# Two layers of the second block moved, for half the tokens, into the expert stage

## The chip, the cores and the metric

The kernel runs on one core of a Trainium2 chip. TensorE (PE) multiplies, VectorE (DVE), ScalarE (ACT) and GpSimd (POOL) do the rest, and SyncE (SP) only issues transfers; each engine runs its own instructions in order, and they meet through semaphores. The metric is the device time of one execution in microseconds (us).

## The reference

256 tokens of width 1024 go through one block with attention and a product-key expert layer, a norm, and then two layers of a second block. All data are float32. What matters here:

```python
# first block, end: 128 experts for each token, drawn from tables of 16384 rows
ub = jnp.take(u_tab, ib, axis=0)
a = jnp.einsum('td,ted->te', xb, ub, preferred_element_type=jnp.float32)
w = gb * jax.nn.gelu(a, approximate=False)
vb = jnp.take(v_tab, ib, axis=0)
return jnp.einsum('te,ted->td', w.astype(vb.dtype), vb)
...
# second block, for each of two layers
h = rmsnorm_2(x, norm_g[l])
z = h @ w_in[l]                      # 1024 -> 2512
...                                  # gated linear attention (gla) and causal attention (mla) with low-rank q, k, v
x = x + jnp.concatenate([o_gla, o_mla], axis=-1) @ w_out[l]
```

Both attentions of the second block are causal: the first 128 tokens need nothing of the last 128, and the last 128 need the keys, the values and the gla state of the first.

## The kernel before

The tokens are two tiles of 128, a token to a partition. After the first block's attention comes the **expert stage**: for each tile 128 turns, in 16 groups of 8 (`GROUP`). In a turn POOL gathers, by an indirect transfer each, one row of `peer_u` and one of `peer_v` for every token (512 KB each, `gather`, L777). DVE multiplies the u row with the token and sums (`product`, L2168), and in between chooses the experts of the next two heads (`choose`). After eight products ACT takes gelu (L1006), DVE multiplies by the gates (`weights`, L2173), ACT makes eight diagonal matrices (`diagonals`, L1013), and PE adds the eight v rows, two products of 128x512 each, into two PSUM banks (`peer_group`, L1538). A float32 product is two matmul instructions, so a turn is 4 of them. The rows have buffers of their own: a set of 8 for u and 8 for v in `wring`, and from group 8 (`DEEP`) on a second set that the even groups use (`second`, L442). `u_rows` and `v_rows` issue a gather as soon as the same buffer's last row is used: one group back for groups 0 to 7, two groups back after them. POOL alternates u of group n+1 with v of group n.

When tile 0's experts are done, DVE and ACT finish its sums and norms beside the first turns of tile 1 (`finish_tile_0`). The last four v rows of all are added by DVE (`last_experts`).

Then comes the **tail**: `layer(l)` twice on every engine, both tiles together. PE's order is written out by hand: transposes of the normed rows (`zT`, L1240), the projections of `w_in` (`gqk`, L1252; `c`, `gv`, `gg`, `mg`, L1582), the low-rank products (`uq`, `ukv`, L1620, L1624), gla's chunks, the scores (`ms`, L1734, L1738), `mPT`, `mPV`, and the output product (`y2`, L1582). PE alternates the tiles, so that it has one tile's products while ACT, DVE and POOL work on the other. ACT sums squares and empties PSUM, POOL turns sums of squares into inverse roots (`inverse_rms`, L816, L820), DVE does norms, rotations, masks and residuals. The layer's weights come in eight loads on SP (`layer_chunk`) into the four places of `wring`; each waits for the last use of the load before it in its place (`LAST2`). One layer's loads are (2512 + 1024) x 1024 floats of `w_in` and `w_out`, 256 x 768 of `w_uq` and 128 x 1024 of `w_ukv`: 15.8 MB. POOL loads a layer's gains (`load_gains`), 1920 floats broadcast to 128 partitions, 0.98 MB.

## Time and profile before

| what | us |
|---|---|
| median of 3 runs (1134.6 to 1135.64) | 1134.78 |
| span of the profiled execution | 1133.4 |
| DVE's products of tile 1, first to last | about 525 to 851 |
| PE starts on the last tile's normed rows (tail) | 876.69 |
| the last product of PE ends | 1130.2 |

The table is read from the trace: times are us from the first instruction of the profiled execution. The median lies 1.4 above the span.

### The profile page before, as it was taken

The numbers are of one execution on the slowest core, as the hardware profiler recorded it, in microseconds if no ns is written. First come the engines' busy times: TensorE is split into PE (matmuls) and PEld (weight loads), VectorE is DVE, ScalarE is ACT, GpSimd is POOL, SyncE is SP. The second block draws the span as 40 slices with busy tenths as digits, with TensorE's granted clock in tenths as the row PEclk, the third lists the DMA queues.
The fourth block names the chain that finished last, engine by engine and source line by source line (L and its number), as shares of the span: only waits on it lengthen the run. The fifth ranks groups of instructions, "written<-read, shape, count | busy, mean of one in ns | idle before, by whom it ended". The sixth has DMA issues, their size and how long they took to land.

```text
span 1133.4 us, 11178 instructions
## 1 busy us (share of the span) xinstructions
PE 990.1 (87%) x3267; PEld 527.9 (47%) x3267; DVE 653.5 (58%) x1503; ACT 272.5 (24%) x741; POOL 531.0 (47%) x585
## 2 busy tenths in 40 slices
PE   4999999999997877878878688787788999999998
PEld 3858656855453323323333233332335645574454
DVE  5867776985765756756767746744444054212522
ACT  4123332222212111111141110201102364115340
POOL 1210010767777777777777777777750012000100
PEclk9999999999999998999989988889899999999999
DMA  9998855999999999999999999999999444134400
GB/s 341 315 391 319 319 203 177 381 374 408 409 409 412 410 413 413 411 413 414 412 412 414 412 410 414 414 410 414 414 410 344 154 148 124 53 121 149 149 1 38
DMA packets 123505, 361.23 MB, mean 319 GB/s; under 512 B 13400, under 2 KB 20192, under 8 KB 123328
## 3 DMA queue, kind: packets, MB, share of 16 engines
q0 software_dynamic: 75808, 275.86, 61.8%
q1 hardware_dynamic: 45280, 84.02, 20.9%
q10 hardware_dynamic: 2368, 0.76, 0.3%
q8 instruction: 22, 0.36, 0.1%
q14 instruction: 27, 0.22, 0.1%
HBM read 359.56 MB, written 1.05 MB: 318 GB/s over the span
## 4 chain that ended last, share of the span: by engine, by line
PE 46%; DMA 26%; POOL 14%; issue 7%; DVE 3%; ACT 2%; SPq 2%; POOLq 0%; DVEq 0%; ACTq 0%
PE bank L1582 14%; DMA wring<-in_peer_u,ids 12%; PE bank L1538 11%; POOL wring L777 8%; PE bank L1271 6%; DMA wring<-in_peer_v,ids 5%; POOL modb L777 3%; PE bank L1348 2%; DMA modb<-in_peer_u,ids 2%; DMA last_row<-in_peer_v,ids 2%; POOL R L777 2%; DMA wring<-in_ada_w 2%; PE bank L1252 2%; DMA wring<-in_w_in 2%; DMA R<-in_peer_u,ids 2%
## 5 line engine op out<-in xcount | busy, mean ns | idle before, releaser
L1538 PE MATMUL bank<-wring,R 128*128 128x512 f32 x496 | 245.2, 652 | 50.2 <-ACT R L1013 43.0
L2168 DVE CUSTOM_DVE_ANT_0 wring<-wring,bank 128x1024 f32<-128x1024 f32 x160 | 195.2, 1220 | 136.6 <-DMA wring<-in_peer_u,ids 135.9
L1538 PEld LDWEIGHTS bank<-wring,R 128*128 128x128 f32 x496 | 100.4, 208 | 192.6 <-issue 138.3
L777 POOL DMA_INDIRECT wring<-in_peer_u,ids x160 | 152.1, 951 | 56.5 <-issue 39.1
L777 POOL DMA_INDIRECT wring<-in_peer_v,ids x160 | 152.0, 950 | 53.0 <-issue 39.3
L1582 PE MATMUL bank<-wring,hT 128*128 128x512 f32 (+1 forms) x384 | 167.4, 589 | 3.0 <-ACT R L1202 2.5
L816 POOL TENSOR_SCALAR small<-small 128x2 f32<-128x2 f32 (+3 forms) x16 | 3.1, 192 | 307.2 <-ACTq L872 163.5
L1538 PE MATMUL bank<-R,modb 128*128 128x512 f32 x192 | 105.2, 709 | 38.6 <-ACT modb L1013 38.2
L1582 PEld LDWEIGHTS bank<-wring,hT 128*128 128x128 f32 x384 | 71.2, 190 | 83.7 <-issue 79.5
L1538 PEld LDWEIGHTS bank<-R,modb 128*128 128x128 f32 x192 | 42.6, 229 | 101.1 <-issue 55.0
L2168 DVE CUSTOM_DVE_ANT_0 modb<-modb,bank 128x1024 f32<-128x1024 f32 x48 | 58.6, 1221 | 44.3 <-DMA modb<-in_peer_u,ids 44.3
L2168 DVE CUSTOM_DVE_ANT_0 R<-R,bank 128x1024 f32<-128x1024 f32 x48 | 58.6, 1221 | 40.8 <-DMA R<-in_peer_u,ids 39.9
L1006 ACT ACTIVATE small<-small 128x8 f32<-128x8 f32 x32 | 6.7, 209 | 312.0 <-DVE small L2168 311.9
L1271 PE MATMUL bank<-hT,wring 128*128 128x256 f32 x304 | 69.8, 388 | 3.9 <-DVE small L1965 1.7
L1271 PEld LDWEIGHTS bank<-hT,wring 128*128 128x128 f32 x304 | 58.1, 194 | 13.5 <-issue 3.1
L1538 PE MATMUL bank<-wring,modb 128*128 128x512 f32 x128 | 57.8, 600 | 7.1 <-DMA wring<-in_peer_v,ids 3.7
L1013 ACT ACTIVATE modb<-const,small 128x128 f32<-128x128 f32 x128 | 39.2, 388 | 76.6 <-DVE small L2173 76.6
L1801 DVE SCALAR_TENSOR_TENSOR modb<-wring,small,modb 128x512 f32<-128x512 f32 x64 | 48.1, 752 | 14.9 <-DMA wring<-in_ada_w 11.4
L1013 ACT ACTIVATE R<-const,small 128x128 f32<-128x128 f32 x124 | 38.0, 388 | 73.0 <-DVE small L2173 73.0
L777 POOL DMA_INDIRECT R<-in_peer_u,ids x48 | 45.8, 953 | 14.6 <-issue 11.6
L777 POOL DMA_INDIRECT R<-in_peer_v,ids x48 | 45.7, 952 | 14.6 <-issue 12.2
L777 POOL DMA_INDIRECT modb<-in_peer_u,ids x48 | 45.5, 949 | 14.6 <-issue 11.9
(315 smaller groups left out, 1278.1 us busy)
## 6 DMA issues: line engine op xcount, KB each, us to landing
wring<-in_w_in SPq DMA_DIRECT2D x12, 2048.0 KB, 13.4
wring<-in_ada_w SPq DMA_DIRECT2D x8, 2048.0 KB, 13.9
...
wring<-in_w_in SPq DMA_DIRECT2D x4, 1024.0 KB, 10.5
...
wring<-in_peer_u,ids POOLq DMA_INDIRECT x160, 11.0
```

The lines of the kernel that those rows point to most:

```text
L777: pool.indirect_dma_start(dst, None, table, bass.IndirectOffsetOnAxis(index, 0)).then_inc(landed, 16)
L816: chain.step(pool.tensor_scalar(sums, sums, 1.0 / dim, EPS, ALU.mult, ALU.add))
L1006: act.activation(g8[:, b, :], a8[:, b, :], ACT.Gelu).then_inc(gelu_ready, 1)
L1013: act.activation(diag[b][:, s, :], ident, ACT.Copy, scale=w8[:, b, s:s + 1]).then_inc(diag_ready, 1)
L1252: last = pe.matmul(pb[:, o:o + P], w[:, k, a:a + P], hT[:, k, t * P:(t + 1) * P], start=k == 0, stop=k == KD - 1)
L1271: last = pe.matmul(pb[:, i * S:(i + 1) * S], w[:, k, a:a + P], hT[:, k, :], start=k == 0, stop=k == KD - 1)
L1348: last = pe.matmul(pb[:, :], hT[:, k, t * P:(t + 1) * P], w[:, k, :], start=k == 0, stop=k == KD - 1)
L1538: last = pe.matmul(pb[half][:, :], diag[b][:, s, :], v_place(n, b, s)[:, half * 512:(half + 1) * 512], start=False, stop=closing and s == ...
L1582: last = pe.matmul(pb[:, 0:n], hT[:, k, t * P:(t + 1) * P], w[:, k, wcol:wcol + n], start=k == 0, stop=k == KD - 1)
L1801: ins = dve.scalar_tensor_tensor(acc, w[:, k, :], csil[:, k:k + 1], before, ALU.mult, ALU.add)
L2168: dve.tensor_tensor_reduce(row, row, h_psum(t), 1.0, 0.0, ALU.mult, ALU.add, a8[:, b, s:s + 1]).then_inc(u_free, 1)
```

## The change

The second block's work is cut into small jobs for one tile and one layer (a "visit" `v`: 0 and 1 are tile 0's layers, 2 and 3 tile 1's). `visit_slots` puts the jobs of a visit on 50 turns, `shadow_schedule` puts visits 0 and 1 on turns 16 to 115 of tile 1's expert stage, and PE, ACT and DVE do a turn's jobs after the turn's expert work; PE's row of a turn is that of ten turns before (`LAG`). Tile 0's last sum and norm go to turns 11 to 15. `tail_schedule` is the order of visits 2 and 3, after the experts, for tile 1 alone.

The weights of both layers are now loaded twice: for visits 0 and 1 by SP into two places (`shadow_ring`) that were the second set of gather buffers, in the order `USED_BY_SHADOW`, and for visits 2 and 3 into `wring` as before. So tile 1's groups (16 and up) have one set of 8 + 8 gather buffers and wait one group back. After the front, which loads layer 0's gains as before, SP loads gains three times (layers 1, 0, 1), where POOL did once; in visits 0 and 1 the inverse roots are ACT's (`inverse_roots`, Ln and Exp), in 2 and 3 POOL's as before. Keys, values and gla's state of tile 0 are kept for tile 1. The core of the diff:

```diff
+LAG = 10
+SHADOW = 16
+VISIT = 50
...
+def visit_slots():
+
+    out = [[] for _ in range(VISIT)]
+
+    def at(r, *jobs):
+        out[r] += jobs
+
+    at(0, ("xsq",))
+    at(2, ("norm",))
+    at(3, ("zT",), ("zTe",))
+    for p in range(4):
+        at(5 + p, ("c", p))
+    at(9, ("ce",), ("gqk", 0))
+    at(10, ("gqk", 1))
+    at(11, ("cn",))
+    at(12, ("cT",), ("cTe",))
+    at(13, ("gqk", 2))
+    at(14, ("gqk", 3))
+    at(15, ("gqke",), ("gl",))
+    at(16, ("gate",), ("u", 0))
+    at(17, ("gated",), ("ue", 0))
+    at(18, ("decays",), ("u", 1))
+    at(19, ("ue", 1))
+    at(20, ("gv", 0), ("glaq",))
+    at(21, ("gv", 1), ("rope", 0))
+    at(22, ("gv", 2), ("keT",), ("rope", 1))
+    at(23, ("gv", 3), ("keR",))
+    at(24, ("gve",), ("A",), ("rope", 2))
+    at(25, ("gg", 0), ("Am",), ("rope", 3))
+    at(26, ("gg", 1), ("U",))
+    at(27, ("gg", 2), ("st",))
+    at(28, ("gg", 3), ("qkt",))
+    at(29, ("gge",), ("qkte",), ("go",))
+    at(30, ("mg", 0), ("gosq",))
+    at(31, ("mg", 1))
+    at(32, ("goe",), ("ms", 0))
+    at(33, ("mg", 2), ("mk", 0), ("mk", 1))
+    at(34, ("mx", 0), ("mx", 1), ("ms", 1))
+    at(35, ("mg", 3), ("mPT", 0))
+    at(36, ("mge",), ("mPTe", 0), ("mPT", 1), ("mk", 2), ("mk", 3))
+    at(37, ("mPTe", 1), ("mx", 2), ("mx", 3), ("mPV", 0), ("cT2", 0))
+    at(38, ("cT2e", 0), ("mPV", 1), ("mPT", 2))
+    at(39, ("mPTe", 2), ("mPT", 3), ("y2", 0, 0))
+    at(40, ("mPTe", 3), ("mPV", 2), ("y2", 0, 1))
+    at(41, ("mPV", 3), ("y2", 1, 0))
+    at(42, ("moe",), ("y2", 1, 1))
+    at(43, ("cT2", 1))
+    at(44, ("cT2e", 1))
+    at(45, ("y2", 0, 2))
+    at(46, ("y2", 0, 3))
+    at(47, ("y2", 1, 2), ("y2e", 0))
+    at(48, ("y2", 1, 3))
+    at(49, ("y2e", 1))
+    return out
+
+
+def shadow_schedule():
+
+    out = [[] for _ in range(SLOTS + LAG)]
+    for at, *jobs in ((11, ("experts", 0, 0)), (12, ("experts", 0, 1)), (13, ("final squares", 0)), (15, ("final", 0))):
+        out[at] += jobs
+    for v in range(LAYERS):
+        for r, jobs in enumerate(visit_slots()):
+            out[SHADOW + v * VISIT + r] += [(kind, v, *rest) for kind, *rest in jobs]
+    return out
+
+
+def tail_schedule():
+
+    out = []
+    for v in range(LAYERS, NT * LAYERS):
+        def to(*jobs):
+            out.extend((kind, v, *rest) for kind, *rest in jobs)
+
+        to(("xsq",), ("rms", 0), ("norm",), ("zT",), ("zTe",))
+        to(*[("c", p) for p in range(4)], ("ce",), ("rms", 1), ("cn",))
+        to(*[("gqk", i) for i in range(4)], ("cT",), ("cTe",), ("gqke",), ("gv", 0), ("gl",), ("u", 0), ("u", 1))
+        to(("gate",), ("gated",), ("ue", 0), ("ue", 1), ("rms", 2), ("decays",), ("rope", 0), ("glaq",))
+        to(*[("gv", p) for p in range(1, 4)], ("gve",), ("rope", 1), ("rope", 2), ("rope", 3))
+        to(*[("gg", p) for p in range(4)], ("gge",), ("keT",), ("keR",), ("A",), ("Am",), ("qkt",), ("qkte",))
+        to(("mg", 0), ("mg", 1), ("ms", 0), ("mk", 0), ("mk", 1), ("mx", 0), ("mx", 1), ("U",), ("st",))
+        to(("mPT", 0), ("mPTe", 0), ("mPT", 1), ("mPTe", 1), ("ms", 1), ("mk", 2), ("mk", 3), ("mx", 2), ("mx", 3))
+        to(("mg", 2), ("mPV", 0), ("mPV", 1), ("go",), ("gosq",), ("rms", 3), ("goe",), ("mPT", 2), ("mPTe", 2), ("mPT", 3), ("mPTe", 3))
+        to(("mg", 3), ("mge",), ("mPV", 2), ("mPV", 3), ("moe",), ("cT2", 0), ("cT2e", 0))
+        to(*[("y2", ch, p) for ch in range(2) for p in range(2)], ("cT2", 1), ("cT2e", 1))
+        to(("y2", 0, 2), ("y2", 0, 3), ("y2e", 0), ("y2", 1, 2), ("y2", 1, 3), ("y2e", 1))
+    return out
+
...
 
-            return b % 2 == 0 and (not isinstance(n, int) or n >= DEEP)
+            return b % 2 == 0 and (not isinstance(n, int) or DEEP <= n < NG // NT)
 
         def u_place(n, b, s):
...
                 eng.wait_ge(sems[s], 16 * (n + 1))
+            elif isinstance(n, int) and n >= NG // NT:
+                eng.wait_ge(sems[s], 16 * (n + 1 - DEEP // 2))
             else:
                 eng.wait_ge(sems[s], pair * 16 + 16 * (DEEP // 2 + 1))
...
+        shadow_ring = [region(0, 4096), region(10592, 4096)]
+        USED_BY_SHADOW = [1, 0, 3, 2, 4, 5, 6, 7]
...
+            def next_gains(v):
+
+                sp.wait_ge(gains2_used, v + 1)
+                load_gains(sp, (v + 1) % LAYERS, gains2_landed)
+
+
+            for v in range(LAYERS):
+                for j, n in enumerate(USED_BY_SHADOW):
+                    place = shadow_place(n, v)[0]
+                    if v == 0 and j == 0:
+                        sp.wait_ge(v_free, (NG // NT - 1) * GROUP)
+                    elif v == 0 and j == 1:
+                        sp.wait_ge(u_free, (NG // NT - 1) * GROUP)
+                    else:
+                        before = USED_BY_SHADOW[j - 2]
+                        await_full(sp, last_use(before, v if j >= 2 else v - 1))
+                    layer_chunk(n, v, shadow_ring[place], shadow_landed[place])
+                    if n == 6:
+                        next_gains(v)
+            sp.wait_ge(x_ready, X_BEFORE[1] + 1)
+            sp.dma_start(out[0, 0:P, :], xrow[:, 0, :]).then_inc(out_done, 16)
 
 
             sp.wait_ge(u_free, NG * GROUP)
+            for n in (1, 0):
+                layer_chunk(n, 0, wring[:, n, :], w_landed[n])
+            await_full(sp, ("peer", NT - 1, 1))
+            layer_chunk(2, 0, wring[:, 2, :], w_landed[2])
+            sp.wait_ge(x_ready, NT + 5)
+            layer_chunk(3, 0, wring[:, 3, :], w_landed[3])
+            for v in range(LAYERS, NT * LAYERS):
+                for n in (5, 4, 6):
+                    await_full(sp, last_use(n - 4, v))
+                    layer_chunk(n, v - LAYERS, wring[:, n - 4, :], w_landed[n - 4])
+                await_full(sp, last_use(3, v))
+                layer_chunk(7, v - LAYERS, wring[:, 3, :], w_landed[3])
+                if v == LAYERS:
+                    next_gains(v)
+                    for n in (1, 0, 2, 3):
+                        await_full(sp, last_use(n + 4, v))
+                        layer_chunk(n, 1, wring[:, n, :], w_landed[n])
...
-                    pool.wait_ge(u_free, (n - (1 if n < DEEP else 2)) * GROUP + s + 1)
+                    pool.wait_ge(u_free, (n - (2 if DEEP <= n < NG // NT else 1)) * GROUP + s + 1)
...
-                    pool.wait_ge(v_free, (n - (1 if n < DEEP else 2)) * GROUP + s + 1)
+                    pool.wait_ge(v_free, (n - (2 if DEEP <= n < NG // NT else 1)) * GROUP + s + 1)
...
+            def tail_step(kind, v, *i):
+
+                if kind != "rms":
+                    return
+                n, t = 5 + 4 * (v - LAYERS) + i[0] + 1, v // LAYERS
+                if i[0] == 0:
+                    inverse_rms(n, (ss[:, 4 + t:5 + t], rstd[:, 4 + t:5 + t], D))
+                elif i[0] == 1:
+                    inverse_rms(n, (ss[:, 6 + t:7 + t], rstd[:, 6 + t:7 + t], QR), (ss[:, 8 + t:9 + t], rstd[:, 8 + t:9 + t], KVR))
+                elif i[0] == 2:
+                    inverse_rms(n, (ssh, rstdh, QK))
+                else:
+                    inverse_rms(n, (ssg, ssg, GDV))
+
+            for job in tail_schedule():
+                tail_step(*job)
...
+            def inverse_roots(*norms):
+
+                for sums, _, dim in norms:
+                    chain.step(act.activation(sums, sums, ACT.Ln, scale=1.0 / dim, bias=eps))
+                chain.wait()
+                for n, (sums, dst, _) in enumerate(norms):
+                    last = act.activation(dst, sums, ACT.Exp, scale=-0.5)
+                    if n < len(norms) - 1:
+                        chain.step(last)
+                return last
+
+            def square_sum(src, junk, total):
+                chain.link(act.activation(junk, src, ACT.Square, accum_out=total))
+
+            def summed(v, *norms):
+
+                if v < LAYERS:
+                    inverse_roots(*norms).then_inc(shadow_rms_ready, 1)
                 else:
-                    squares([xrow[:, t, :]], [t], spent_row(t))
+                    act.sem_inc(squares_ready, 1)
...
+            for slot, jobs in enumerate(shadow_schedule()):
+                done = slot - GROUP
+                if done >= 0 and done % GROUP == 0 and done < SLOTS:
+                    gelu(NG // NT + done // GROUP, (done // GROUP) % 2)
+                if done >= 0 and done % GROUP == 1 and done < SLOTS:
+                    n = NG // NT + done // GROUP
+                    diagonals(n, n % 2, rows=CLOSING if n == NG - 1 else GROUP)
+                if slot % (GPP * GROUP) == 13 and slot < SLOTS - GPP * GROUP:
+                    exponentials_of_gates(PIECES // NT + slot // (GPP * GROUP) + 1)
+                for kind, *rest in jobs:
+                    if kind == "final squares":
+                        act.wait_ge(x_ready, NT + 1)
+                        rms([xrow[:, 0, :]], D, [0], spent_row(0))
+                    else:
+                        layer_step(kind, *rest)
+            act.wait_ge(x_ready, NT + 5)
+            squares([xrow[:, 1, :]], [1], spent_row(1))
+            for job in tail_schedule():
+                layer_step(*job)
...
+            def peer_row(n, b, t, s, pair=None, last_row=False):
...
+            for slot, jobs in enumerate(shadow_schedule()):
+                row = slot - LAG
+                if 0 <= row < SLOTS - (GROUP - CLOSING):
+                    n = NG // NT + row // GROUP
+                    peer_row(n, n % 2, 1, row % GROUP, last_row=row == SLOTS - (GROUP - CLOSING) - 1)
+                for job in jobs:
+                    layer_step(*job)
+            for job in tail_schedule():
+                layer_step(*job)
...
+            def beside(k, b, s):
+                for job in schedule[((k - half) * GPP + b) * GROUP + s]:
+                    layer_step(*job)
+
+            for k in range(half, PIECES):
+                piece(k, 1, k < PIECES - 1, beside=beside)
             release_rows(1)
+            for jobs in schedule[SLOTS:]:
+                for job in jobs:
+                    layer_step(*job)
 
```

The jobs themselves (`layer_step` on PE, ACT and DVE, `rotate`) hold the instructions of the old `layer` for one tile: 128 columns where two tiles had 256.

## Rows read from the trace of the kernel before

**Rows 1.** The page: the span, and DMA's busy tenths in 40 slices.

```profile
span 1133.4 us, 11178 instructions
...
DMA  9998855999999999999999999999999444134400
```

**Rows 2.** Windows: busy us of each engine (instructions), granted clock, DMA share, GB/s.

```profile
260.00:340.00 80.00, 76.48 (x232) 41.06 (x231) 53.14 (x130) 16.88 (x45) 60.29 (x65) 1.00 1.03 409
...
525.00:863.00 338.00, 272.11 (x545) 110.24 (x544) 207.44 (x462) 64.02 (x173) 240.73 (x254) 0.90 1.03 410
...
877.00:999.00 122.00, 119.50 (x495) 66.73 (x493) 37.12 (x94) 44.89 (x135) 12.01 (x18) 1.00 0.38 125
999.00:1133.00 134.00, 128.67 (x555) 73.95 (x553) 38.40 (x95) 43.80 (x133) 7.43 (x10) 1.00 0.24 88
```

**Rows 3.** The waits: who waited for whom, total, times, longest.

```profile
DVE wring L2168 <- DMA wring<-in_peer_u,ids: 135.9, 136, 2.3
```

**Rows 4.** Timeline in tile 1's expert stage: two of DVE's products in a row.

```profile
842.19 1.22 DVE L2168 CUSTOM_DVE_ANT_0 wring<-wring,bank 128x1024 f32<-128x1024 f32 x1 [1.34 <-DMA wring<-in_peer_u,ids]
...
844.74 1.22 DVE L2168 CUSTOM_DVE_ANT_0 wring<-wring,bank 128x1024 f32<-128x1024 f32 x1 [1.32 <-DMA wring<-in_peer_u,ids]
```

**Rows 5.** DMA issues, median us to landing: from 260 to 340, then 790 to 850.

```profile
wring<-in_peer_v,ids POOLq DMA_INDIRECT x33, 7.4
...
wring<-in_peer_v,ids POOLq DMA_INDIRECT x16, 18.8
```

**Rows 6.** The chain that ended last, end of the expert stage and tail.

```profile
841.98 21.36 DMA wring<-in_peer_v,ids
...
876.69 1.09 PE bank L1240 x8
...
995.41 3.44 PE bank L1582 x8
998.84 7.14 PE bank L1252 x64
1005.99 3.12 PE bank L1582 x8
...
1112.73 17.45 PE bank L1582 x40
```

**Rows 7.** Windows (columns as in rows 2) with loads of SP and POOL.

```profile
66.00:72.00 6.00, 6.00 (x21) 2.85 (x20) 3.28 (x6) 0.60 (x1) 0.00 (x0) 1.00 1.05 415
...
126.00:132.00 6.00, 6.00 (x16) 2.66 (x16) 5.51 (x12) 1.09 (x4) 0.00 (x0) 1.00 1.05 387
...
852.00:860.00 8.00, 8.00 (x26) 4.01 (x25) 0.75 (x1) 1.93 (x5) 0.00 (x0) 1.00 1.05 378
...
956.00:972.00 16.00, 15.03 (x70) 8.77 (x70) 3.69 (x18) 6.67 (x20) 4.58 (x8) 1.00 0.69 182
```

**Rows 8.** Timeline and groups of the tail: ACT, DVE, POOL steps.

```profile
904.69 1.28 ACT L1141 ACT_TABLE_LOAD   x1
905.98 0.63 ACT L1141 ACTIVATE modb<-modb 128x512 f32<-128x512 f32 x1
...
925.77 0.96 DVE L2348 TENSOR_TENSOR R<-R,small 128x768 f32<-128x768 f32 x1 [5.88 <-POOLq L822]
...
931.05 0.42 DVE L2373 TENSOR_TENSOR R<-R,small 128x256 f32<-128x256 f32 x1
...
988.55 1.06 ACT L871 ACTIVATE R<-xrow 128x1024 bf16<-128x1024 f32 x1 [7.59 <-DVEq L2465]
...
991.02 1.28 DVE L2239 SCALAR_TENSOR_TENSOR hrow<-xrow,small,gains 128x1024 f32<-128x1024 f32 x1 [2.56 <-POOLq L822]
...
L820 POOL TENSOR_TENSOR small<-small 128x8 f32<-128x8 f32 x2 | 3.3, 1634 | 0.4 <-POOL small L816 0.4
```

**Rows 9.** Windows where PE stands and starts again (columns as in rows 2).

```profile
860.00:864.00 4.00, 0.88 (x3) 0.05 (x1) 3.13 (x3) 0.00 (x0) 0.00 (x0) 0.98 0.65 183
864.00:868.00 4.00, 3.79 (x21) 3.79 (x22) 3.67 (x4) 0.00 (x0) 0.00 (x0) 0.59 0.86 282
```

More of the change, by code:

```diff
@@ new lines, in left @@
+def left(kind, v, *i):
+    if kind in ("ce", "gqke", "cTe", "gve", "gge", "mge"):
+        return [(kind[:-1], v)]
+    if kind == "gated":
+        return [("gl", v)]
+    if kind == "keR":
+        return [("keT", v)]
+    if kind == "zTe":
+        return claimed("zT", v)
+    if kind == "ue":
+        return claimed("u", v, i[0])
+    if kind == "Am":
+        return claimed("A", v)
+    if kind == "goe":
+        return claimed("go", v)
+    if kind == "st":
+        return claimed("U", v)
+    if kind == "qkte":
+        return claimed("qkt", v)
+    if kind == "mk":
+        return [("ms", v, i[0])]
+    if kind == "moe":
+        return [("mo", v)]
+    if kind in ("mPTe", "cT2e", "y2e"):
+        return [(kind[:-1], v, i[0])]
+    return []
@@ L205, in plan_banks, with plan_layers @@
+def plan_layers(b, jobs, idle):
+    idle = list(idle)
+    for kind, v, *i in jobs:
+        for name in claimed(kind, v, *i):
+            b.plan(name, idle.pop(0))
+        for name in left(kind, v, *i):
+            idle.append(b.jobs[name][0])
 def plan_banks():
@@ L1564, in _ @@
-                if t == 1:
-                    peer_group(NG - 2, 0, t)
-                    transpose_tile("zT", 0, 4 * NT, 0)
-                    peer_group(NG - 1, 1, t, closing=True)
-                for half in range(2 if t == 0 else 0):
-                    pb = bank[banks.jobs[("peer", t, half)][0]]
-                    full(pe.matmul(pb[:, :], zeros, hrow[:, t, half * 512:(half + 1) * 512], start=False, stop=True,
-                                   skip_group_check=True), ("peer", t, half))
@@ new lines, in _ @@
+            pe.wait_ge(ids_ready, 1)
+            pe.wait_ge(zeros_set, 1)
+            open_sums(0)
+            for n, jobs in enumerate(late_router()):
+                peer_group(n, n % 2, 0)
+                for job in jobs:
+                    router_step(job)
+            for n in range(len(late_router()), DEEP):
+                peer_group(n, n % 2, 0)
+            with pe.Fori(DEEP // 2, NG // 4) as m:
+                for b in range(2):
+                    peer_group(m * 2 + b, b, 0, m)
@@ L2470, in _ @@
-            with dve.Fori(0, LAYERS - 1) as l:
-                chain.loop(l, 58)
-                layer(l)
-                chain.end_loop(LAYERS - 1)
-            layer(LAYERS - 1, last=True)
+            for job in tail_schedule():
+                layer_step(*job)
 _INS = ["x", "c", "ada_w", "ada_b", "norm1_g", "w_in", "na_rpb", "out_norm_na_g", "out_norm_dil_g", "w_out", "norm2_g",
```

1230 lines of the change are left out of this document (567 added, 663 removed).

## The prediction, on record before the change was run

> **What bounds the kernel now.** I read the page, then the windows by stage, then the waits and the timeline of the expert stage, and last the chain that ended last. On the page DMA is busy in every slice of the expert stage and falls to 4 tenths or less after it [rows 1]. The windows say how full it is: share 1.03 at 409 to 410 GB/s, early and in tile 1 alike, while DVE is busy 207.4 of 338 us and PE 272.1 [rows 2]. DVE's first wait is for u rows [rows 3]. A turn takes 844.74 - 842.19 = 2.55 us, and half of it DVE stands until the next u row lands [rows 4]. A gather's landing time grows from 7.4 to 18.8 us [rows 5], so POOL issues them faster than they land. The expert stage is bound by transfers.
>
> The tail is another kernel. PE is busy 119.5 of 122 us in its first layer and 128.7 of 134 in its second, at the full granted clock (2.4 GHz), with DMA at 0.38 and 0.24 [rows 2]. It runs from 876.69 to the end of the span, 256.7 us [rows 1, 6], and is bound by PE.
>
> So the change moves PE work out of a stage that PE bounds into one with room on PE. But the moved layers bring transfers with them, and there is no room for these.
>
> **What the stage pays.** *Loads.* Visits 0 and 1 load 2 x 15.8 = 31.6 MB, none of which could replace a later load, since visits 2 and 3 load the same again. SP's loads alone run at 387 GB/s with a share of 1.05: full [rows 7] (second row). 31.6 MB / 0.387 = 81.7 us. Bounds: with the dil bias of POOL beside a load of SP, 415 GB/s were moved [rows 7] (first row): 76; with the last gathers beside the first layer loads 378 [rows 7] (third row): 84. I take 82, the plain load.
>
> *Gains.* Two of the three loads of gains fall in the stage. In 956 to 972 one such load and a part of a weight load used 0.69 x 16 = 11.0 us of DMA for 182 x 16 = 2.9 MB [rows 7] (fourth row). Without its 0.98 MB, 1.9 MB at 387 take 5.2 us at share 1.05, so gains take about 5.6, two 11. By bytes alone at 410 it would be 5. Tile 0's output, 0.5 MB, adds 1. I take 12, bounds 6 and 12. Loads and gains: 94.
>
> *The second set of gather buffers.* With one set a gather waits for the row one group back. The window 260 to 340 is a stretch of groups with one set, and it moves 409 GB/s [rows 2], as much as with two. I cost it at nothing while turns flow. At the end it costs: v of the last group waits for PE's rows of the group before, ten turns behind DVE. PE does those eight at 4 instructions of 0.43 us (3.44 / 8 [rows 6]), 1.72 a row, 14 us after the last `weights` but one; a landing of 7.4 us follows [rows 5]. Bytes alone for what is then open (8 v rows and some 6 u rows, 7.3 MB at 410) would be 18 us. So about 4 us, bounds 0 and 8.
>
> *PE, DVE and ACT beside the rows.* One layer of one tile costs PE: `gv`, `gg`, `mg` 24 steps of 0.86, `y2` 16 of 0.86, `c` 8 of 0.78, `gqk` 7.14 [rows 6], 47.8 us; transposes, low-rank products, gla and attention bring it to a quarter of what both layers take for both tiles. That is (119.5 + 128.7 [rows 2] + 10.5 of tile 0 hidden before 876.69) / 4 = 65; tile 1 about 65.5, tile 0, with half the scores, 63. Over the 100 turns of the visits PE has 100 x 1.99 (272.11 x 4 / 545 [rows 2], clock dips in it) + 126 = 325 us. DMA has 100 x 2.55 + 94 = 349. PE fits, at 93 per cent. DVE has 207.4 / 128 = 1.6 us a turn and (37.1 + 38.4) / 4 = 19 us a visit [rows 2], 0.4 a turn, under 3.5. ACT has (44.9 + 43.8) / 4 = 22 us a visit [rows 2] and a table load of 1.28 us [rows 8] at each change between gelu, Exp, Ln and Silu; some 20 of these a visit are still under the 175 us of 50 turns.
>
> What is new are waits: PE's jobs now stand in one queue with the rows. If `cT` waits for `cn`, row n waits behind it, its v buffer stays taken, POOL stands at that v gather and the next u gathers stand behind it. A u gather goes out some 6 turns, 21 us, ahead of its product; less a landing of, say, 12 (between the 7.4 and 18.8 of [rows 5]) a slip up to 9 us is absorbed. Bounds: 0 if all is absorbed. From above, a visit strung out as in the single-tile tail below (82 us) with 50 rows of 1.99 between takes 182 us in place of 175, 14 us for two, and twice that if DVE's products and ACT's diagonals are held up as well: 28. I take 11. With the drain of 4: 15, bounds 0 and 36.
>
> The stage grows by 94 + 15 = 109 us.
>
> **What the tail gives back.** PE keeps 65.5 us a layer. It loses the other tile as cover, so I follow one layer from the first transpose. ACT empties `zT` late: 1.0 idle. `c`, `gqk` cover the squares and POOL's roots; `cT`, `gv`, `gl` and the low-rank products follow without a stop. Then ACT has gate (two table loads, 1.28 each), `ue` 0 and 1, POOL a root of 8 columns of 1.63 us, DVE the rotation of 5.7 us (925.77 to 931.47) [rows 8] and `glaq`. `gv` and `gg` (12 us) cover all but 2.1 before `qkt`. The first exponentials with their table load: 2.7. In DVE's list `goe` stands before `mPTe` 2 and 3, so heads 2 and 3 wait behind gla's squares, POOL and norm: 4.5. `cT2e`, twice: 1.5. Together 11.8. Between the layers come the residual 0.7, squares 1.06 to the norm's start 991.02 - 988.55 = 2.5, the norm 1.28 [rows 8] and steps between engines: 4.9, where today the other tile's `y2` runs.
>
> After standing for some 3 us PE started again at a mean granted clock of 0.59, a mix of 1.2 and 2.4 GHz, for 4 us [rows 9], some 1.5 us lost. Three such stands: 4.5. The last part, from PE's last product at 1112.73 + 17.45 = 1130.2 [rows 6] to 1133.4 [rows 1], stays: 3.2. The weights of `gg` are asked for at the end of `gqk` and needed 12 us later, as long as 2 MB and a part of another take; I cost this at nothing, up to 5 us.
>
> Tail: 2 x (65.5 + 11.8) + 4.9 + 3.2 + 4.5 = 167, after rounding up for the steps 168. Bounds: 148 if half the stands are filled (139 is PE's floor with the residual chain), 182 with more waits and weights late. It gives back 256.7 - 168 = 89, bounds 75 and 109.
>
> The row shows a table load of 1.28 us and the activation right behind it, 905.98 - 904.69 = 1.29 [rows 8]. The Trainium skill, ScalarE: Activation LUTs, section What ACT_TABLE_LOAD costs, puts a drain of about 1.38 us beside the 1.28. By that page the tail would be an estimated 8 us longer (three loads a layer lie open on the path) and the sum 1163; the row shows no drain, and the sum goes by the row.
>
> **The sum.** 1133.4 + 94 + 15 - 89 = 1153.4; the median stands 1.4 above the span, so 1155 us, 1.8 per cent slower.
>
> **Rivals.** *A, the forecast:* transfers cost the stage more than PE saves in the tail, 1136 to 1178. Chance 0.58.
>
> *B, the queues lock:* each visit's waits between PE, DVE and ACT hold back rows, buffers and gathers more than I allow, DMA falls below 1.0 within the visits, and the stage grows by 140 to 170: 1178 to 1215, middle 1195. For it: PE at 93 per cent, one queue for all. Against: 6 turns of slack. Chance 0.14.
>
> *C, the other side: the tail comes near PE's floor.* If ACT's and DVE's chains hide behind `gv`, `gg` and `mg` and the tail takes 140 to 147 us, it gives 110 to 117 and the kernel takes 1134.8 + 109 - 113 = 1131, less where the stage's waits vanish too: 1115 to 1132. It decides from a tail of 147 us down at a stage of +109. For it: today PE stands only some 8 us in both layers [rows 2]. Against: that is with two tiles. Chance 0.16.
>
> *D, the loads ride free:* SP's loads take room that the gathers leave, and the stage is set by PE, 128 x 1.99 + 126 = 381 against 327 us, +54: 1133.4 + 54 + 15 - 89 + 1.4 = 1115. For it: 415 GB/s was moved once with both queues. Against: a share over 1 in every full window, and landings that grow [rows 5]. Chance 0.07. The Trainium skill, DMA: Bandwidth & Descriptors, section Specifications, gives a ceiling of 435 GB/s; by it the stage would grow by an estimated 60. The windows read here stop at 415 [rows 7], so they do not bear that ceiling out.
>
> *E, a draw* within 0.2 per cent (2.3 us, about what a measurement here can tell from no change): 0.05.
>
> **Chances and range.** Faster: C and D, 0.23. Same: 0.05. Slower: A and B, 0.72. The range leaves out D's lower half and B's upper: 1117 to 1195, and the likeliest case alone spans 1136 to 1178.
>
> **What would show it.** Right: in the profile after, tile 1's stage at DMA share 1.0 throughout and about 109 us longer, with its turns in the visits at 3.4 to 3.6 us; DVE waiting for u rows as before; a tail near 168 us with PE idle before `qkt`, heads 2 and 3 and `xsq`. Wrong: DMA at 0.9 or less within the visits (B), GB/s above 430 there (D), or PE busy over 95 per cent of a tail under 150 (C).

## The result, and the profile after

The changed kernel takes 1145.12 us (median) against 1135.2 of the kernel before (four runs each): a ratio of 1.0096, 95% interval 1.0067 to 1.0125, slower by one per cent. The profiled execution took 1145.04 us with a span of 1143.1, so the spans differ by 9.7 us. The forecast was 1155.

The page of the changed kernel: span, granted clock, DMA's busy tenths and GB/s in 40 slices.

```profile
span 1143.1 us, 11280 instructions
...
PEclk9999999999998888878899899899999896998999
DMA  9998955999999999999999999999999999438440
GB/s 343 327 392 293 348 198 174 392 378 407 409 409 412 411 412 414 412 411 401 409 410 409 406 409 400 342 402 409 408 408 398 410 408 346 171 124 282 160 148 19
```

The stretch in which DMA is full has grown by two to three slices [rows 1], and no slice moves more than 414 GB/s. Windows of the changed kernel, columns as in [rows 2]: the expert stage of tile 1, a part of the first visit's end, and the two layers of the tail.

```profile
525.00:952.00 427.00, 380.16 (x1092) 179.75 (x1092) 243.26 (x576) 147.99 (x361) 243.14 (x254) 0.95 1.02 401
...
720.00:740.00 20.00, 19.67 (x44) 8.93 (x45) 6.71 (x12) 0.81 (x2) 9.27 (x10) 0.88 0.85 312
...
965.08:1056.24 91.16, 77.02 (x306) 43.48 (x307) 21.14 (x57) 29.09 (x77) 5.22 (x10) 0.89 0.54 192
1056.24:1143.10 86.86, 74.17 (x306) 43.86 (x306) 19.90 (x56) 28.16 (x75) 4.51 (x8) 0.92 0.31 113
```

The stage runs at 401 GB/s where it ran at 410 [rows 2]. The tail's clock is 0.89 and 0.92 where it was 1.00 in both layers [rows 2]. DVE's waits and products in the visits answer to [rows 3] and [rows 4]; first the waits from 571 to 940, then the products from 640 to 890 (shortest, median and longest in ns, first and last start).

```profile
DVE wring L2322 <- DMA wring<-in_peer_u,ids: 114.5, 73, 3.1
```

```profile
L2322 DVE CUSTOM_DVE_ANT_0 wring<-wring,bank x70: 1190/1221/1223, 642.4 to 886.4; 128x1024 f32<-128x1024 f32 x70
```

DVE still waits for u rows above all, and a turn takes (886.4 - 642.4) / 69 = 3.54 us. PE in the tail, from the first layer and then from the second (from 1056.24 on): start, us, line, operation, idle time before it and what ended that.

```profile
965.08 1.97 PE L1768 MATMUL bank<-const,hrow 128*128 128x128 f32 x8 [15.12 <-DVE hrow L2396]
967.78 9.54 PE L1758 MATMUL bank<-wring,hT 128*128 128x464 f32 x16 [0.73 <-issue]
...
1006.74 1.09 PE L1861 MATMUL bank<-const,R 128*128 128x128 f32 x8 [2.11 <-DVEq L2560]
...
1008.11 5.29 PE L1758 MATMUL bank<-wring,hT 128*128 128x512 f32 x8
...
1030.93 0.49 PE L1897 MATMUL bank<-early,pT 128*128 128x128 f32 x2 [4.18 <-DVE pT L2496]
...
1033.59 9.72 PE L1758 MATMUL bank<-wring,hT 128*128 128x512 f32 x16 [0.69 <-ACT hT L1389]
...
1044.43 7.13 PE L1758 MATMUL bank<-wring,hT 128*128 128x512 f32 x16 [0.69 <-ACT hT L1389]
1056.24 1.97 PE L1768 MATMUL bank<-const,hrow 128*128 128x128 f32 x8 [4.68 <-DVE hrow L2396]
1058.94 8.34 PE L1758 MATMUL bank<-wring,hT 128*128 128x464 f32 x16 [0.73 <-issue]
...
1096.72 1.89 PE L1861 MATMUL bank<-const,R 128*128 128x128 f32 x8 [2.13 <-DVEq L2560]
...
1120.89 0.79 PE L1897 MATMUL bank<-early,pT 128*128 128x128 f32 x2 [4.18 <-DVE pT L2496]
...
1124.50 7.13 PE L1758 MATMUL bank<-wring,hT 128*128 128x512 f32 x16 [0.69 <-ACT hT L1389]
```

PE's waits from 965 to 1143 that these lines don't give: who waited for whom, us in total, times, longest.

```profile
PE bank L1758 <- ACT hT L1389: 2.7, 4, 0.7
PE bank L1890 <- ACT R L1384: 2.1, 4, 0.8
```

In the first layer two runs of 16 equal matmuls of `y2` stand side by side: 9.72 us behind the stand of 4.18, 7.13 behind a short one. The extra time is clock, not idle time. A stand does not cost the same each time: in the second layer `y2` takes 7.13 behind the same stand, and the low clock falls on the short matmuls ahead of it (0.79 us in place of 0.49).

The two sides of the sum, forecast and measured:

| term | forecast | measured |
|---|---|---|
| stage: start of the tail's transposes, against 876.69 [rows 6] | +109 | 965.08 - 876.69 = +88.4 |
| - loads, gains, output | 94 | 427 us at 401 less 338 at 410 [rows 2] is 32.7 MB; at 410: 80 |
| - slower flow of all bytes, end of the stage | 15 | 427 - 171.2 / 0.410 = 9 |
| tail, to the span's end | 168 | 1143.1 - 965.08 = 178.0 |
| - PE's work at the full clock | 131 | 77.02 x 0.89 + 74.17 x 0.92 = 136.8 |
| - low clock | 4.5 | 151.2 - 136.8 = 14.4 |
| - PE idle, between the layers and the end included | 31.7 | 178.0 - 151.2 = 26.8 |

The tail gives back 256.7 - 178.0 = 78.7, and 88.4 - 78.7 = 9.7. Both sides were smaller than forecast, the stage by 21 us and the gift of the tail by 10.

### The profile page after: what moved, and what is told of

Read it like the earlier page. It is cut to its first block, busy times and chain, and to the rows that moved or that the text cites. A ratio compares the mean times of both kernels' runs of the same rounds, so it can differ in the third digit from the quotient of the medians.

```text
span 1143.1 us, 11280 instructions
## 1 busy us (share of the span) xinstructions
PE 993.9 (87%) x3307; PEld 538.3 (47%) x3307; DVE 654.8 (57%) x1543; ACT 323.7 (28%) x812; POOL 525.0 (46%) x575
## 4 chain that ended last, share of the span: by engine, by line
PE 55%; DMA 23%; issue 7%; POOL 5%; DVE 4%; ACT 4%; SPq 2%; DVEq 0%; POOLq 0%; ACTq 0%
PE bank L1710 21%; PE bank L1758 13%; DMA wring<-in_peer_u,ids 10%; PE bank L1444 7%; DMA R<-in_w_in 5%; POOL wring L969 3%; PE bank L1779 3%; PE bank L1521 2%; DMA wring<-in_peer_v,ids 2%; DMA wring<-in_ada_w 2%; DMA wring<-in_w_in 2%; SPq L867 1%; PE bank L1434 1%; ACT R L1282 1%; POOL R L969 1%
## 5 line engine op out<-in xcount | busy, mean ns | idle before, releaser
L2322 DVE CUSTOM_DVE_ANT_0 wring<-wring,bank 128x1024 f32<-128x1024 f32 x224 | 272.6, 1219 | 206.0 <-DMA wring<-in_peer_u,ids 203.0
L969 POOL DMA_INDIRECT wring<-in_peer_v,ids x224 | 214.0, 955 | 171.9 <-PE bank L1710 90.7
L969 POOL DMA_INDIRECT wring<-in_peer_u,ids x224 | 214.2, 956 | 76.1 <-issue 54.4
L1710 PE MATMUL bank<-wring,modb 128*128 128x512 f32 x384 | 180.8, 607 | 18.4 <-DMA wring<-in_peer_v,ids 10.3
L1710 PEld LDWEIGHTS bank<-wring,R 128*128 128x128 f32 x496 | 98.9, 204 | 151.2 <-issue 131.8
L1710 PEld LDWEIGHTS bank<-wring,modb 128*128 128x128 f32 x384 | 70.9, 193 | 108.9 <-issue 84.3
L1758 PE MATMUL bank<-R,hT 128*128 128x512 f32 (+1 forms) x192 | 96.1, 626 | 22.5 <-issue 11.3
L1758 PE MATMUL bank<-wring,hT 128*128 128x512 f32 (+1 forms) x192 | 94.3, 645 | 4.2 <-ACT hT L1389 2.7
L1758 PEld LDWEIGHTS bank<-R,hT 128*128 128x128 f32 x192 | 37.6, 200 | 69.0 <-issue 59.4
L1444 PEld LDWEIGHTS bank<-hT,wring 128*128 128x128 f32 x304 | 58.0, 194 | 12.9 <-DMA wring<-in_w_in 2.7
L1758 PEld LDWEIGHTS bank<-wring,hT 128*128 128x128 f32 x192 | 39.2, 211 | 50.6 <-issue 44.1
L1955 DVE SCALAR_TENSOR_TENSOR modb<-wring,small,modb 128x512 f32<-128x512 f32 x64 | 48.1, 751 | 14.2 <-DMA wring<-in_ada_w 10.7
L1710 PE MATMUL bank<-R,modb 128*128 128x512 f32 x64 | 39.6, 787 | 14.4 <-ACT modb L1208 14.4
## 6 DMA issues: line engine op xcount, KB each, us to landing
wring<-in_ada_w SPq DMA_DIRECT2D x8, 2048.0 KB, 13.9
```

The source lines that it names most:

```text
L969: pool.indirect_dma_start(dst, None, table, bass.IndirectOffsetOnAxis(index, 0)).then_inc(landed, 16)
L1444: last = pe.matmul(pb[:, i * S:(i + 1) * S], w[:, k, a:a + P], hT[:, k, :], start=k == 0, stop=k == KD - 1)
L1710: last = pe.matmul(pb[half][:, :], diag[b][:, s, :], v_place(n, b, s)[:, half * 512:(half + 1) * 512], start=False, stop=last_row, skip_gr ...
L1758: last = pe.matmul(pb[:, 0:n], hT[:, k, cols], w[:, k, 0:n], start=k == 0, stop=k == KD - 1)
L1955: ins = dve.scalar_tensor_tensor(acc, w[:, k, :], csil[:, k:k + 1], before, ALU.mult, ALU.add)
L2322: dve.tensor_tensor_reduce(row, row, h_psum(t), 1.0, 0.0, ALU.mult, ALU.add, a8[:, b, s:s + 1]).then_inc(u_free, 1)
```

## Experiments on the stage

**half_loads and eighth_loads: what the bytes cost, and where PE takes over.** The layers' inner loops stay whole; only the bytes loaded for them shrink. The edit, with 4 of 8 row blocks (eighth_loads: 1, and chunk 1 whole):

```diff
-                    sp.dma_start(dst.rearrange("p (k m) -> p k m", k=KD), chunk_dram(w, l, a, a + 512)).then_inc(s, 16)
+                    sp.dma_start(dst.rearrange("p (k m) -> p k m", k=KD)[:, 0:K, :], chunk_dram(w, l, a, a + 512)[:, 0:K, :]).then_inc(s, 16)
...
-                    layer_chunk(n, v, shadow_ring[place], shadow_landed[place])
+                    layer_chunk(n, v, shadow_ring[place], shadow_landed[place], 4)
```

> The changed kernel, with the visits' loads of chunks 0, 1, 2, 4, 5, 6 and 7 cut to the first four of their eight row blocks; the other half of each weight is what lies in the buffer, so part of the layers' weights is wrong for tile 0. 14.5 MB less. Theory (bytes through full DMA engines set the stage): 14.5 MB at 410 GB/s is 35 us, at the 387 of my forecast 37, so about 1109 against 1145 of the changed kernel. Rival (PE's matmuls and the waits of its one queue set the visits, and the loads ride beside them): 1138 to 1145.

> As half_loads, but chunk 1 whole and chunks 0, 2, 4, 5, 6 and 7 cut to one row block of eight (the rest of these weights is wrong). 22.0 MB less. By bytes alone 54 us at 410 GB/s: 1091. But PE is busy 336 of the 369 us from 571 to 940 of the changed kernel, some 13 of them through its lower clock, so I expect PE to become the bound after 33 to 46 us: 1099 to 1112, with DMA under 1.0 in the visits. Rival (no cover by transfers at all, PE and queues set the visits): 1138 to 1145.

Measured: half_loads 1110.58 us, ratio 0.978 (0.9766 to 0.9794); eighth_loads 1109.31, 0.9773 (0.9758 to 0.9787). Windows of half_loads, then of eighth_loads, in the visits (both profiled executions are the shortest of their kernel, 1104.71 and 1104.87):

```profile
640.00:740.00 100.00, 100.00 (x308) 47.86 (x307) 68.55 (x177) 37.42 (x83) 62.24 (x65) 1.00 1.02 397
740.00:890.00 150.00, 146.60 (x465) 72.55 (x464) 87.30 (x188) 57.71 (x150) 95.44 (x100) 1.00 1.03 407
```

```profile
640.00:740.00 100.00, 98.72 (x304) 47.00 (x303) 69.79 (x179) 37.43 (x83) 61.95 (x64) 1.00 0.97 364
740.00:890.00 150.00, 150.00 (x474) 74.50 (x473) 87.82 (x192) 59.11 (x154) 95.25 (x101) 1.00 1.00 383
```

Half the bytes took 34.5 us away, what 14.5 MB take at 420 GB/s, so the bytes set the changed kernel's visits. With half of them gone PE is already busy 246.6 of these 250 us, while DMA is still full (1.02 and 1.03). The next 7.5 MB gave 1.3 us, less than the intervals can tell from nothing: PE is busy 248.7 of the 250 us, at the full clock, and DMA falls to 364 and 383 GB/s. That floor is 35.8 us below the changed kernel, a stage of 88.4 - 35.8 = 53 us over the kernel before (the tail is as long: 1103.1 - 925.33 = 177.8), next to the 54 that rival D worked out for a stage set by PE.

**no_gains: the small broadcast loads.**

```diff
                     if n == 6:
-                        next_gains(v)
```

(with the waits for them taken out where tile 0's second layer and tile 1's first begin).

> The changed kernel without the two loads of gains between the visits and the tail (16 DMAs of SP): tile 0's second layer uses the first layer's gains, which changes its values alone. My forecast's term of 11 us for both (DMA time of small broadcast rows): 1134. Rival (their bytes alone, 2 x 0.98 MB at 410 GB/s): 5 us, 1140. If SP's time at these loads is what delays the last weight chunk and with it PE's stand of 7.6 us at 720, 1137 or less.

Measured: 1140.54, ratio 1.0057 (1.0035 to 1.008), 4.6 us under the changed kernel, with intervals that just overlap. The value lies at the bytes' 5 us; the forecast's 11 is at the edge of what the intervals leave.

**one_set_before: the second set of buffers alone, in the kernel before.**

```diff
-                    pool.wait_ge(v_free, (n - (1 if n < DEEP else 2)) * GROUP + s + 1)
+                    pool.wait_ge(v_free, (n - (2 if DEEP <= n < NG // NT else 1)) * GROUP + s + 1)
```

and the same line for `u_free`.

> The kernel before, with one part of the change alone: in tile 1 POOL waits for the row one group back, as if the second set of gather buffers were gone (the buffers still alternate). My forecast: 0 while turns flow, and 4 us at the end of the stage (0 to 8): 1135 to 1143, middle 1139. Rival (the depth of the buffers is what keeps DMA full): turns longer by a tenth of a landing or more, 10 us up: 1145 and above.

Measured: 1135.13, ratio 0.9998 (0.9989 to 1.0007). In the kernel before, the second set is worth nothing that shows. But there PE's rows do not run ten turns behind, so this run does not try the end of the changed kernel's stage. The traces do. DVE's last product in the kernel before, and in the changed kernel the last v row from issue to landing:

```profile
849.86 1.22 DVE L2168 CUSTOM_DVE_ANT_0 wring<-wring,bank 128x1024 f32<-128x1024 f32 x1 [1.32 <-DMA wring<-in_peer_u,ids]
```

```profile
943.91 7.82 DMA wring<-in_peer_v,ids
```

From the end of the last product to the landing of the last v row the kernel before takes 863.34 [rows 6] - 851.08 = 12.3 us, the changed kernel 951.73 - 941.03 = 10.7 (its last product is shown with loads_held). The one set costs nothing there. Within the stage POOL stands 82.1 us at v gathers for PE to leave a buffer (571 to 952; 3.7 us in the kernel before, 525 to 863), with DMA full but for the dip below. Whether a second set would have bridged that dip is not tested.

**y2_later: the dip at 720.** In the first visit PE stands ahead of `y2`'s second block; from the timeline of the changed kernel:

```profile
720.33 3.75 PE L1758 MATMUL bank<-R,hT 128*128 128x512 f32 x4 [7.58 <-issue]
```

The trace names no releaser, but SP issued weight chunk 7 at 697.27, and this load took 23.0 us to land, which is 720.3. In the second visit it is the same: issued at 865.96, 23.9 us to landing, and PE goes on at 889.95. The dip to 0.85 follows the first of the two. The edit moves that block behind the landing:

```diff
-    at(41, ("mPV", 3), ("y2", 1, 0))
-    at(42, ("moe",), ("y2", 1, 1))
+    at(41, ("mPV", 3))
+    at(42, ("moe",))
...
-    at(47, ("y2", 1, 2), ("y2e", 0))
-    at(48, ("y2", 1, 3))
-    at(49, ("y2e", 1))
+    at(47, ("y2", 1, 0), ("y2e", 0))
+    at(48, ("y2", 1, 1), ("y2", 1, 2))
+    at(49, ("y2", 1, 3), ("y2e", 1))
```

> The changed kernel with the first half of y2's second block six turns later in each visit, behind the landing of weight chunk 7. Theory (PE's stands of 7.6 us at 720 and 3.75 us at 890 hold the rows, their buffers and then the gathers, and cost the dip of DMA to 0.85 in 720 to 740, 4.8 us of bytes): 1140. Rival (the visit's end moves as much later as the stand was, or the dip is absorbed by what is queued): 1144 to 1147.

Measured: 1145.48, ratio 1.0087 (1.0074 to 1.0101): no gain that shows. Windows of y2_later at the place of the dip and over the stage, and POOL's last gather:

```profile
720.00:740.00 20.00, 20.00 (x50) 9.06 (x49) 11.72 (x23) 1.84 (x6) 13.16 (x14) 0.98 1.04 405
...
525.00:952.00 427.00, 381.14 (x1097) 179.45 (x1095) 244.27 (x578) 148.01 (x361) 246.58 (x257) 0.96 1.03 405
```

```profile
945.39 0.94 POOL L969 DMA_INDIRECT wring<-in_peer_v,ids  x1 [1.59 <-PE bank L1710]
```

The dip is gone, 405 GB/s in place of 312. But the last three v gathers now each wait 1.6 us (1.61, 1.63, 1.59) for PE to leave a buffer, where in the changed kernel only the last waits, 1.14 us, and the last of all goes out at 945.39 in place of 943.91. So the bytes that were ahead are given back at the end. The rival's second form held.

**loads_held: the tail's first loads behind the last v row.**

```diff
             sp.wait_ge(u_free, NG * GROUP)
+            rows_landed(sp, v_landed, NG - 1, (NG - 1) % 2, GROUP - 1)
```

> The changed kernel with SP's first two weight loads of the tail held until the last v row has landed; today they start at 941.1 and share the engines with 4.5 MB of gathers still to come, the last of which lands at 951.8. Theory (the end of the stage waits for bytes that aren't needed before 965): 4.5 MB from 938 at 410 GB/s end at 949, 2.5 us less: 1142.5. Rival (the gathers' own latency sets it, or chunk 1 comes late for c): 1145 to 1148.

Measured: 1146.63, ratio 1.0093 (1.0079 to 1.0108), the same as the changed kernel. The profiled execution is the shortest of the five, 1140.62. DVE's last product and its last v rows, in the changed kernel and then in loads_held:

```profile
939.81 1.22 DVE L2322 CUSTOM_DVE_ANT_0 wring<-wring,bank 128x1024 f32<-128x1024 f32 x1 [1.33 <-DMA wring<-in_peer_u,ids]
...
951.82 1.28 DVE L2596 SCALAR_TENSOR_TENSOR wring<-wring,small 128x1024 f32<-128x1024 f32 x1 [0.20 <-DMA wring<-in_peer_v,ids]
```

```profile
938.84 1.22 DVE L2323 CUSTOM_DVE_ANT_0 wring<-wring,bank 128x1024 f32<-128x1024 f32 x1 [1.33 <-DMA wring<-in_peer_u,ids]
...
947.86 3.92 DVE L2597 SCALAR_TENSOR_TENSOR wring<-wring,small 128x1024 f32<-128x1024 f32 x3 [0.52 <-DMA wring<-in_peer_v,ids]
```

From the last product to the end of these steps: 13.3 us, and 951.8 - 938.84 = 12.9 with the loads held. The 2.5 us that I expected are not there; in these two executions the loads hold the last rows back by 0.4 us at most.

## Experiments on the tail

**warm: matmuls of no use while PE waits.**

```diff
+                def keep_busy(pb, n):
+                    for _ in range(n):
+                        pe.matmul(pb[:, :], ident, const[:, 384:896], start=True, stop=True)
...
+                    if v >= LAYERS:
+                        keep_busy(claim(pe, ("zT", v, 0)), 24 if v == LAYERS else 8)
                     pe.wait_ge(rows_ready, ROWS_BEFORE[v] + 1)
...
+                    if v >= LAYERS:
+                        keep_busy(claim(pe, ("qnT", v)), 4)
                     pe.wait_ge(rotated, v + 1)
```

> The changed kernel with matmuls of no use in tile 1's two layers, into a bank that the next job overwrites, where PE waits: 24 ahead of the first layer's transposes (15.1 us of waiting), 8 ahead of the second's (4.7 us), 4 ahead of each qkt (2.1 us). Nothing of the output changes. Theory (the tail is longer than forecast because PE's granted clock stays low for many us after each stand: 0.89 and 0.92 over the layers, some 8 us a layer): the transposes, c and mg run at the full clock, 2 x 5 us less: about 1135. Rival (the matmuls of the tail are long for another reason, weights or banks, or the low clock is a rule of its own that no activity lifts): 1144 to 1147.

Measured: 1149.42, ratio 1.0128 (1.0107 to 1.015), 4.3 us above the changed kernel, with intervals that overlap. PE at the start of the first layer and, last, of the second, in warm:

```profile
953.92 20.76 PE L1764 MATMUL bank<-const 128*128 128x512 f32 x48
974.52 1.04 PE L1774 MATMUL bank<-const,hrow 128*128 128x128 f32 x8
976.35 6.46 PE L1758 MATMUL bank<-wring,hT 128*128 128x464 f32 x16 [0.78 <-ACT hT L1302]
...
1061.74 1.04 PE L1774 MATMUL bank<-const,hrow 128*128 128x128 f32 x8
```

`c` takes 6.46 in place of 9.54, the transposes 1.04 in place of 1.97: the clock came back. But the 24 matmuls are 48 records and last 20.76 us, longer than the 15.1 us that they were to fill, and PE was still in them for 5.0 us after DVE's norm (968.27 to 969.56) was done. So warm tested the clock and a delay together. From the norm's end to the span's end it takes 178 us, as the changed kernel does; the rest of its loss lies before the norm, which starts at 968.27 in place of 963.74. Why, these runs do not tell; in goe_later, warm_fitted and order_later, whose stage is that of the changed kernel, it starts at 965.7 to 967.2, so some of it is the spread between executions.

**goe_later, and all_three.** The edit of goe_later, one line of the tail's order:

```diff
-        to(("mg", 2), ("mPV", 0), ("mPV", 1), ("go",), ("gosq",), ("rms", 3), ("goe",), ("mPT", 2), ("mPTe", 2), ("mPT", 3), ("mPTe", 3))
+        to(("mg", 2), ("mPV", 0), ("mPV", 1), ("go",), ("gosq",), ("rms", 3), ("mPT", 2), ("mPTe", 2), ("mPT", 3), ("mPTe", 3), ("goe",))
```

all_three joins warm, goe_later and y2_later, each as above.

> The changed kernel with goe behind mPTe 2 and 3 in the order of the tail's jobs, so that heads 2 and 3 no longer wait on DVE behind gla's squares, roots and norm. Theory (the 4.2 us of PE's stand at 1026 and 1116 is DVE's order, and cT2 can't follow before goe, 2.6 us after PE's next work): 2 x 1.5 us less, and some clock back: 1140 to 1142. Rival (goe sets the chain anyway, cT2 waits for it): 1144 to 1146.

> warm, goe_later and y2_later in one. If the three prices are separate: 1145 - 10 - 4 - 5 = 1126, faster than both kernels. If only the clock counts: 1135, level with the kernel before. If none does: 1145.

Measured: goe_later 1143.42, ratio 1.0066 (1.005 to 1.0082); all_three 1142.69, 1.0068 (1.0054 to 1.0083). PE in goe_later, at the place of the stand of 4.18 us:

```profile
1031.77 0.66 PE L1912 MATMUL bank<-const,hrow 128*128 128x128 f32 x4 [2.70 <-DVEq L2480]
1033.11 8.72 PE L1758 MATMUL bank<-wring,hT 128*128 128x512 f32 x16 [0.69 <-ACT hT L1389]
```

Heads 2 and 3 no longer wait, but `cT2` waits 2.70 us for `goe`, as expected, and `y2` behind it still takes 8.72. The prices of all_three did not add up to the 1126 expected. In it PE is late for the first transposes as in warm (970.53, with the norm done at 965.80), y2_later had no gain to bring, and in its second layer `y2` still takes 9.80 behind a stand of 2.70. Neither kernel is clear of the changed one: the intervals overlap.

**warm_fitted, order_later, best.** warm_fitted has warm's numbers cut to 16, 4 and 2. order_later moves a quarter of `mg` too:

```diff
-        to(("mg", 2), ("mPV", 0), ("mPV", 1), ("go",), ("gosq",), ("rms", 3), ("goe",), ("mPT", 2), ("mPTe", 2), ("mPT", 3), ("mPTe", 3))
+        to(("mPV", 0), ("mPV", 1), ("go",), ("gosq",), ("rms", 3), ("mPT", 2), ("mPTe", 2), ("mPT", 3), ("mPTe", 3), ("mg", 2), ("goe",))
```

best joins both with loads_held.

> As warm, with the matmuls of no use cut to what fits into PE's waits, at the 0.865 us that one took there: 16 (13.8 of 15.1 us), 4 (3.5 of 4.7 us) and 2 (1.7 of 2.1 us). Theory (the low clock after stands costs the tail some 14 us; warm gave the clock back and lost more than that to its own length): the tail falls from 178 to about 168, 1135. Rival (the matmuls ahead cost what the clock gives): 1143 to 1147.

> goe_later, and mg's third quarter behind the last transposes of probabilities too, so that gla's output product starts 1.7 us earlier and covers less of the wait for goe. Theory (the stand of 2.7 us ahead of cT2 that goe_later left is the chain from go, so an earlier go shortens it): 2 x 1.7 us less than goe_later's 1143.4: 1140. Rival (heads 0 and 1 aren't ready that early, PE stands there instead): 1143 or more.

> warm_fitted, order_later and loads_held in one. If the three prices add: 1145 - 10 - 5 - 2.5 = 1127.5, faster than the kernel before (1135). If the clock alone counts: 1135. Neither: 1141 or more.

Measured, with the tail of the profiled execution from the first transposes to the span's end, and the granted clock of its two layers:

| kernel | us | ratio to before (95%) | tail | clock |
|---|---|---|---|---|
| changed | 1145.12 | 1.0096 (1.0067 to 1.0125) | 178.0 | 0.89, 0.92 |
| warm_fitted | 1142.64 | 1.0061 (1.0048 to 1.0074) | 1141.1 - 967.0 = 174.1 | 0.91, 0.96 |
| order_later | 1139.49 | 1.0039 (1.0024 to 1.0053) | 1136.5 - 968.5 = 168.0 | 0.92, 0.93 |
| best | 1128.63 | 0.9944 (0.9925 to 0.9963) | 1126.8 - 967.9 = 158.9 | 1.00, 0.98 |

PE in warm_fitted, the start of the first layer and the place of the stand that is left there:

```profile
951.25 13.90 PE L1764 MATMUL bank<-const 128*128 128x512 f32 x32
967.02 1.09 PE L1774 MATMUL bank<-const,hrow 128*128 128x128 f32 x8 [1.88 <-DVE hrow L2404]
968.90 9.53 PE L1758 MATMUL bank<-wring,hT 128*128 128x464 f32 x16 [0.79 <-ACT hT L1302]
...
1030.35 0.80 PE L1905 MATMUL bank<-early,pT 128*128 128x128 f32 x2 [4.18 <-DVE pT L2504]
1033.96 10.08 PE L1758 MATMUL bank<-wring,hT 128*128 128x512 f32 x16 [0.69 <-ACT hT L1389]
```

PE in order_later at the same place:

```profile
1031.59 0.66 PE L1912 MATMUL bank<-const,hrow 128*128 128x128 f32 x4 [0.98 <-DVEq L2480]
1032.93 7.13 PE L1758 MATMUL bank<-wring,hT 128*128 128x512 f32 x16 [0.69 <-ACT hT L1389]
```

PE in best, and the windows of its two layers:

```profile
969.74 6.47 PE L1759 MATMUL bank<-wring,hT 128*128 128x464 f32 x16 [0.78 <-ACT hT L1303]
...
1027.15 7.13 PE L1759 MATMUL bank<-wring,hT 128*128 128x512 f32 x16 [0.69 <-ACT hT L1390]
```

```profile
967.86:1047.22 79.36, 73.72 (x319) 42.12 (x319) 21.23 (x57) 28.97 (x77) 5.23 (x10) 1.00 0.63 222
1047.22:1126.80 79.58, 71.98 (x310) 41.27 (x310) 19.99 (x56) 27.81 (x75) 4.51 (x8) 0.98 0.40 143
```

Shortening the stand from 4.18 to 0.98 us gives its own 3.2 us and the low clock behind it: `y2` takes 10.08 with the one, 7.13 with the other. In the changed kernel, warm and warm_fitted each of the six stands of 4.18 is followed by a low clock (about 0.5), for 3.5 to 10.5 us; none of the four of 0.98 in order_later and best is. warm_fitted alone missed its 168: the first `c` stayed at 9.53, and the stand behind `go` still cost its clock. Matmuls in the waits and the shorter chain together bring the clock to 1.00 and 0.98 and the tail to 158.9, 19.1 less, where the two apart gave 178.0 - 174.1 = 3.9 and 10.0. These are one execution each. best beats both kernels: 0.56 per cent under the kernel before, 16.5 us under the changed one, with runs from 1124.57 to 1134.63. order_later is clear of the changed kernel as well, warm_fitted is not. What loads_held adds to best was not tried apart, and why best's runs lie so far apart is open.

## Why the prediction was right, and where it was off

**The bound, and the side.** Right: the stage is bound by transfers, the tail by PE, and transfers cost more (88.4) than the tail gives (78.7). That the sum is only 10 us off is in part luck: the cost was forecast 21 us too high and the gift 10 too high, and these cancel. half_loads shows the first; the tail's rows show PE busy 151.2 of 178 us. DMA stayed at 1.02 over the stage, turns at 3.54 us lie in the forecast's 3.4 to 3.6.

**"I take 82, the plain load", and gains of 11.** Mis-sized. A load of SP alone moved 387 GB/s [rows 7], but loads and gathers together move 401 over the stage, so all that was added, 32.7 MB, costs 80 at the rate of gathers alone, with 9 for the slower flow of all, and not 94. The gains cost about 4.6 (no_gains), near their bytes; that the DMA time read from the window [rows 7] (fourth row) does not count beside gathers is argued.

**The second set.** Nothing while turns flow: right. "So about 4 us" at the end: wrong, the way from the last product to the last v row is 10.7 us where it was 12.3, and one_set_before measures nothing.

**Coupling of the queues, 11.** Near in number, by luck in part: the flow at 401 in place of 410 is worth 9 us. Of these 20 - 20 x 312 / 410 = 4.8 are the dip at 720. Its cause was not among the waits named: the late landing of chunk 7 in the first visit held PE. The rest is no wait that shows: the other 407 us moved (171.2 - 6.2) / 407 = 405 GB/s, and y2_later, without the dip, moves 405 at a share of 1.03. That mixed transfers run a little slower with the engines full was not in this term. Removing the dip (y2_later) gave nothing in the end, since buffers came free late at the end of the stage.

**Rivals B and D.** DMA did not fall within the visits but for 20 us at 0.85, so B did not come. For D, its condition did not come: no 10 us of the stage moved over 415 GB/s. The Trainium skill, DMA: Bandwidth & Descriptors, section Specifications, gives a ceiling of 435 GB/s; no run here shows that. But D's price for a stage that PE sets came close (54 forecast, 53 with an eighth of the bytes), in part by luck: its 1.99 us a turn hold low clock [rows 2], and eighth_loads ran its visits at 1.00.

**"65.5 PE" a layer.** Too small by 3: 68.5 and 68.2 at the full clock, and best, with six added matmuls of 0.865 us in its first layer's window, has 73.7 - 5.2 = 68.5. A quarter of the work of both tiles leaves out that short matmuls do not halve with the columns; that is argued, not tried.

**The stands of the tail.** The places were right: 2.11 ahead of `qkt` (forecast 2.1), 4.18 behind `goe` (4.5), twice 0.69 at `cT2e` (1.5), 4.68 between the layers (4.9), 0.73 behind `zT` (1.0). Only the exponentials were cheaper, 1.1 in place of 2.7. `gg`'s weights never made PE wait. DVE's order as the cause of the 4.18 is shown by goe_later and order_later.

**"Three such stands: 4.5."** This is the step that failed in the tail. The low clock costs 14.4 us. From [rows 9] I took 1.5 us a stand and three stands. The rows show low clock behind six, the 15.12 ahead of the tail, the 4.68 between the layers, and 2.1 and 4.18 in each layer, at a mean of 2.4 us: 3.1 us for one `c` (9.54 against 6.46 or 6.47), 2.6 for one `y2` (9.72 against 7.13), 1.7 for one `mg` behind 2.11 (5.29 against the 3.60 that eight matmuls of 512 columns take in best at 1042.38). warm and best show that it is the clock, since the same matmuls become short.

**Table loads.** Two loads a layer lie on ACT's path at the gate. In the changed kernel, what stands ahead of ACT's load, the load, and what follows it:

```profile
987.36 0.63 ACT L1325 ACTIVATE modb<-bank,small 128x128 f32<-128x128 f32 x2 [1.25 <-PE bank L1796]
988.00 1.28 ACT L1328 ACT_TABLE_LOAD   x1
989.30 0.42 ACT L1328 ACTIVATE modb<-modb 128x256 f32<-128x256 f32 x1
```

The load starts as the activation ahead of it ends, and 989.30 - 988.00 = 1.30, as in [rows 8]. The Trainium skill, ScalarE: Activation LUTs, section What ACT_TABLE_LOAD costs, adds a drain of about 1.38 us to the load; this trace does not show it, ahead of the load or behind it.

**Rival C.** A tail of 147 us or less did not come, and not in best either (158.9). But best's sum shows how near the sign was: at a stage of +88.4, any tail under 168.3 makes the change a gain.
